# GpSimd's residual update at each sub-layer border placed behind VectorE's last add for the second token tile

## The reference

```python
for i in range(DEPTH):                                            # DEPTH = 2
    f1 = swiglu_ffn(rms_norm(h, ffn1_norm_pre[i]), ffn1_w_gu[i], ffn1_w_down[i])
    h = h + 0.5 * rms_norm(f1, ffn1_norm_post[i])
    u = rms_norm(h, mix_norm_pre[i])
    ...                       # four causal mixers (two attentions, two convolutions), gated and summed
    h = h + rms_norm(merged @ w_o[i], mix_norm_post[i])
    f2 = swiglu_ffn(rms_norm(h, ffn2_norm_pre[i]), ffn2_w_gu[i], ffn2_w_down[i])
    h = h + 0.5 * rms_norm(f2, ffn2_norm_post[i])
    pg = jax.nn.sigmoid(rms_norm(h, ple_norm_gate[i]) @ w_ple_gate[i])
    h = h + pg * rms_norm(p[i] @ w_ple[i], ple_norm_post[i])
```

## Time and profile before

| | |
|---|---|
| time, median of three runs | 1393.84 us (1391.57 to 1394.92) |
| span of the profiled execution | 1392.9 us, which is 0.94 us below that median |
| TensorE, matmuls | 1293.5 us busy, 93% of the span |
| VectorE | 823.9 us, 59% |
| ScalarE | 657.4 us, 47% |
| GpSimd | 254.2 us, 18% |
| mean granted TensorE clock | 0.975 |

### The profile page before, as it was taken

One profiled execution on the slowest core, in us unless ns is written; L12 is line 12 of the kernel. 1 busy time (PEld: TensorE's weight loads), 2 busy tenths in 40 slices (PEclk: granted clock), 3 DMA queues, 4 the chain that ended last, 5 costly groups with the idle time before them and its releaser, 6 DMA issues.

```text
span 1392.9 us, 17344 instructions
## 1 busy us (share of the span) xinstructions
PE 1293.5 (93%) x5972; PEld 1057.9 (76%) x5972; DVE 823.9 (59%) x767; ACT 657.4 (47%) x706; POOL 254.2 (18%) x210
## 2 busy tenths in 40 slices
PE   5299999899999989999969999989999998999996
PEld 4178887788778778888758888878887776888874
DVE  4154555455898765445656554564479886554464
ACT  3144444655645454444455444455664535444444
POOL 3030001310033460000433000040102256100015
PEclk9699999999999999999989999999999999999999
DMA  7675554635545446555257555555554544655641
GB/s 198 149 238 193 182 181 157 220 122 190 173 161 188 151 169 202 183 193 196 91 196 245 192 192 181 181 174 180 177 168 141 190 156 158 207 181 187 201 155 46
DMA packets 156842, 245.29 MB, mean 176 GB/s; under 512 B 9250, under 2 KB 108648, under 8 KB 156776
## 3 DMA queue, kind: packets, MB, share of 16 engines
q1 hardware_dynamic: 152280, 239.22, 51.4%
q0 software_dynamic: 1040, 2.10, 1.4%
q10 hardware_dynamic: 3456, 3.15, 0.8%
HBM read 241.29 MB, written 3.15 MB: 175 GB/s over the span
## 4 chain that ended last, share of the span: by engine, by line
PE 58%; issue 23%; POOL 6%; DVE 5%; DMA 4%; ACT 3%; SPq 0%; POOLq 0%; ACTq 0%; DVEq 0%
PE ps L1239 55%; DMA rel_scratch<-bandD 3%; PE ps L1286 3%; DVE hg L786 2%; POOL h L1139 1%; ACT whi L461 1%; DVE wlo L751 1%; POOL st L1134 1%; DVE hg L780 1%; POOL S L1139 1%; POOL st L1136 1%; DMA raw<-in_ffn_w_gu 1%; POOL hg L1139 1%; ACT gates L470 1%; ACT hg L470 0%
## 5 line engine op out<-in xcount | busy, mean ns | idle before, releaser
L751 DVE TENSOR_TENSOR wlo<-raw,whi 128x2048 fp32r<-128x2048 f32 (+1 forms) x216 | 507.5, 2352 | 348.4 <-ACT whi L461 181.4
L1239 PE MATMUL ps<-whi,xhi 128*128 128x512 f32 (+1 forms) x1280 | 502.9, 401 | 50.0 <-DVE S L795 32.9
L1239 PE MATMUL ps<-wlo,xhi 128*128 128x512 f32 (+1 forms) x1280 | 490.6, 391 | 0.0
L1239 PE MATMUL ps<-whi,xlo 128*128 128x512 f32 (+1 forms) x1280 | 490.4, 391 | 0.0
L1239 PEld LDWEIGHTS ps<-whi,xhi 128*128 128x128 f32 x1280 | 243.1, 191 | 106.6 <-DVE S L795 35.0
L461 ACT ACTIVATE whi<-raw 128x2048 fp32r<-128x2048 f32 (+1 forms) x120 | 225.7, 1884 | 146.6 <-PE ps L1239 98.2
L1239 PEld LDWEIGHTS ps<-whi,xlo 128*128 128x128 f32 x1280 | 243.8, 190 | 51.5
L1239 PEld LDWEIGHTS ps<-wlo,xhi 128*128 128x128 f32 x1280 | 244.4, 191 | 47.7
L467 ACT ACTIVATE whi<-raw 128x2048 fp32r<-128x2048 f32 x96 | 183.5, 1911 | 100.9 <-PE ps L1239 100.9
L1134 POOL TENSOR_TENSOR st<-st,epsc 128x1 f32<-128x1 f32 x36 | 28.3, 787 | 735.6 <-ACT hg L470 665.5
L1239 PE MATMUL ps<-whi,yhi 128*128 128x512 f32 x448 | 142.5, 393 | 1.2 <-DVE ylo L755 0.8
(11 more groups left out here) (127 smaller groups left out, 822.6 us busy)
## 6 DMA issues: line engine op xcount, KB each, us to landing
raw<-in_ffn_w_gu SPq DMA_DIRECT2D x176, 512.0 KB, 4.7
raw<-in_w_in SPq DMA_DIRECT2D x104, 512.0 KB, 4.4
raw<-in_ffn_w_down SPq DMA_DIRECT2D x88, 512.0 KB, 3.9
raw<-in_w_o SPq DMA_DIRECT2D x16, 512.0 KB, 3.6
raw<-in_w_ple_gate SPq DMA_DIRECT2D x16, 512.0 KB, 3.6
raw<-in_w_br_d SPq DMA_DIRECT2D x8, 512.0 KB, 3.6
gbias<-in_b_gate ACTq DMA_DIRECT2D x24, 128.0 KB, 3.1
raw<-in_w_in SPq DMA_DIRECT2D x8, 260.0 KB, 2.9
```

The source lines that it names most:

```text
L751: dve.tensor_tensor(d, a, b, ALU.subtract).then_inc(sem("lo_ready"), 1)
L1239: return nc.tensor.matmul(out_, lhsT, rhs, start=start, stop=stop, skip_group_check=True)
```

## The change

In `residual`, between the two factors of the post norm and the first `scale`, GpSimd now waits until VectorE has finished the last of its four adds of this border, the second half of tile 1. Nothing else is changed: no instruction is added or removed beside the wait.

```diff
@@ -1163,6 +1163,7 @@
                         tt(h[:, t, :], h[:, t, :], tmp[:, t, :], ALU.add, f"h{s}_{t}")
 
                     root(s)
+                    after(f"hg{e}_11")
                     scale(0)
                     add(0)
                     scale(1)
```

## The result

| | before | after |
|---|---|---|
| time, median (lowest to highest) | 1394.05 us (1391.57 to 1394.92), 4 runs | 1402.43 us (1400.86 to 1404.77), 4 runs |
| ratio, 95% interval | | 1.0069 (1.0054 to 1.0084) |
| span of the profiled execution | 1392.9 us | 1401.2 us |
| the same kernel once more, beside 23 runs of before | 1393.40 us | 1401.11 us, ratio 1.0058 (1.0045 to 1.0071) |

The change makes the kernel slower, by 7.7 us or 8.4 us between the medians of the two comparisons. The forecast was 1396.8, the range ended at 1400.6, and the chance given to slower was 0.28. In the experiments every run whose span was measured has a time 1.7 to 1.9 us above that span; so the profiled execution of before, with 1392.9, was by that one of about 1394.7, and not an execution 0.94 us quicker than the median.

The account below looks back on a forecast made before the run. TensorE's matmuls bound the kernel (93% busy), and GpSimd's list sets the last wait at the borders; +3.9 at A, -2.3 at B, +1.4 at C gave +3.0 us on the 1392.9 span, so 1396.8 us, range 1392.0 to 1400.6.

Parts of the forecast that it names:

- The list arithmetic: All borders: times of GpSimd's and VectorE's instructions stepped through, the engines excluding each other for whole instructions and taking turns.
- A, the list: Border A: GpSimd's add(1) ends 0.55 us late, so lo(36), TensorE's last wait in front of unit 36, comes late.
- A, the clock: Border A: the longer gap ahead of unit 36 drops TensorE's clock; 1.4 us each, taken between 1.1 and 1.9.
- B: Border B: add(1) ends 0.55 us late, but 1.7 us of slow clock comes back, in each of two layers.
- C: Border C: lo(105) and lo(106) back to back hold up the root's instructions; add(1) 0.7 us late, bounds 0.2 and 0.9.
- B's return: Border B: the slow stretch moves to where TensorE would wait anyway, so 1.7 us comes back; 0 if the clock falls again.
- two rows of shorter gaps: Profile rows behind the gaps ahead of 920.41 (border A) and 503.05 (border B): slow matmuls cost 1.1 and 1.9 us.
- the outer bound of twice the larger: Border A: the clock's cost bounded by nothing below and by twice the larger of 1.1 and 1.9 us above.
- Rival (c): Borders: lo does not keep GpSimd out of scale(1), chain ends 2.2 us earlier at each; -10 us, 1386.6; chance 0.1.
- "same" and "slower": Whole kernel: chances of a time within 0.3%, 4.2 us, of no change (0.61) and of a slower one (0.28).
- Rival (a): Clock charges at A and gives nothing back at B, or stays low for two stretches at A; +7.4, 1401.2; chance 0.25.
- Rival (b): Border A: the clock stays up, or charges little; +0.2 us in all, 1394.0; chance 0.15.

Follow-up runs that it names:

- fill kernel: Changed kernel plus 20 TensorE matmuls, results unused, in the gap in front of unit 36: 1397.36 us, ratio 1.0025 to the kernel before.
- the wait that is already over: Changed kernel with GpSimd's wait, at the same place, on tile 0's last add, which ended 4 us earlier: 1394.18 us, ratio 1.0000 to the kernel before.
- The waits at A, B and C measured alone: Changed kernel with the wait kept at one kind of border only: A 1401.80 us (1.0061), B 1395.28 us (1.0010), C 1395.56 us (1.0017).
- B alone: Changed kernel with the wait kept only at the two borders B: 1395.28 us, ratio 1.0010 (1.0000 to 1.0019) to the kernel before.
- wait behind scale(0): Changed kernel with the wait moved behind scale(0): 1392.89 us, ratio 0.9989; with ScalarE's order turned and SyncE's gain loads two chunks later too: 1378.88 us, 0.9899.

## Why the prediction was wrong

**What held.** The pair of adds takes 1.29 us in all borders (24 adds of 684 to 693 ns). scale(0) starts 2.8 us later than before against tile 1's fused multiply (2.75 foretold), scale(1) is held up by `lo(35)` (4.45 us against about 4.6 foretold), unit 36 comes 0.59 us late on the mean against 0.55, the gap in front of it is 4.93 us against "5 us", border C costs 0.9 us against 0.7, with both root instructions held up as chosen. The list arithmetic, one whole instruction at a time and the turns between the engines, came out within 0.2 us at every place named here. The Trainium skill ("SBUF — State Buffer", "SBUF: two separate sides") calls the shared ports an exclusive lock that a GpSimd instruction and a VectorE one with two SBUF inputs take for a whole instruction; the 4.45 us of scale(1) behind `lo(35)` and the 2.39 us of scale(0) beside the fused multiply, which has one input in PSUM, agree.

**The terms that were mis-sized.** By the stretches of the table above, in us for both layers:

| term | predicted | measured | by |
|---|---|---|---|
| A, the list | 2 x 0.55 | 2 x 0.59 | border A to unit 36 |
| A, the clock | 2 x 1.4 | 2 x 2.03 (1.45 to 2.6) | unit 36 to `D1a`; taken out in the fill kernel |
| B | 2 x (0.55 - 1.7) | 2 x -0.3 | five slow borders of eight |
| C | 2 x 0.7 | 2 x 0.9 | border C to the end |
| sum | +3.0 | +6.4 | |

The step that failed first is B's return, 1.7 us a layer, an error of 1.7 us in the sum: "Those 12 matmuls from 503.05 are slow now because the clock fell" was true of the one execution that was profiled, and taken for a property of the kernel. In that execution both borders B had the slow stretch, and it was a long one (about 1394.7 against a median of 1393.4); the forecast took the whole return off the median. Next, with 1.3 us, is the clock at A, taken between two rows of shorter gaps; the value measured lies above both, though inside the outer bound of twice the larger. With the measured terms the forecast would have been 1393.4 + 6.4 = 1399.8. That is still inside the range; what carried the measured times past its end of 1400.6 is the part that stays open below.

Three numbers of the prediction are off by themselves. The twelve matmuls from 503.05 cost 1.6 us more than fast ones by their starts (4.44 us against 2.86 with the clock up), not 1.9, as 4.61 holds the end of the last one too. Rival (c) takes its -10 from the forecast, although that sum already holds the +3.0; on the base it gives about 1383.6 and not 1386.6. The parts named for "same" and "slower" add up to 0.62 and 0.27, not 0.61 and 0.28.

Rival (a), that the clock charges at A and gives nothing back at B, was the nearest: +7.4, 1401.2, and its sum is within 1.3 us of both medians. It was right in size more than in mechanism, and so by some luck: against the execution profiled, B did give back about 1 us a layer. Rival (b) fell with the windows at 0.50, rival (c) with the 4.45 us.

**What stays open.** The terms explain 6.4 of the 7.7 to 8.4 us (the interval of the first comparison begins at 7.5 us, that of the second at 6.3). The stretch from `D1a` to border B took 77.3 us instead of 76.1 in two of six cases with the wait, but also in kernels without it, so I do not count it. The turn of the loop, from border C to the next border A, takes 233.6 us in the kernel before and 235.7 with the wait that is already over; in the other kernels it goes from 232.6 to 237.0. In the trace of after these two chances and the start add up to 3 us. The waits at A, B and C measured alone sum to 0.0088 against 0.0058 to 0.0069 together, and B alone at +1.0 per mille, where its stretches promise a gain of some 0.6 us, which lies outside its interval; all the intervals are too wide to say whether the terms interact. Moving SyncE's gain load at border C was not tried. Why the clock falls behind one gap and stays up behind another of the same length is not known either.

## What to carry to other kernels

Before an engine is made to wait so that another runs faster, find the last wait of the stretch and see whose list sets it: here the 14.3 us of TensorE's waits for the adds that the change removed came before waits that hung on GpSimd's list, and bought nothing. A wait against a port conflict belongs behind whatever the other engine's operation can run beside; one instruction later turned a loss of 6 per mille into a gain of 1 (0.2 to 2.0). Where a cost in a single profile is a clock state, look at the same place in the other layers and in kernels that don't touch it before it enters a sum as a constant; and a transfer that is hidden now has to be costed again in each version in which the stall that hides it is gone.

## What the runs showed of the hardware

- The length of a gap on TensorE does not decide alone whether the granted clock is at 0.50 behind it. In all 14 traces, for the gaps of 1.4 us and more that stand in front of weight units behind the borders, counted as fallen where matmuls within the first dozen behind the gap start 0.43 us apart instead of 0.23:

| gap, us | where | clock fell |
|---|---|---|
| 1.42 to 1.60 | border B | 0 of 11 |
| 1.82 to 1.84 | border C, unit 107 | 1 of 7 |
| 1.92 to 1.97 | border C, unit 107 | 0 of 8 |
| 1.97 to 2.16 | border B, tile 1, behind the stalled adds | 5 of 5 |
| 2.29 to 2.31 | border B, tile 1, wait behind scale(0) | 0 of 4 |
| 2.49 to 2.54 | border C | 5 of 12 |
| 2.61 to 2.64 | border A, unit 36 | 1 of 2 |
| 4.05 to 4.08 | border B, tile 0 | 12 of 12 |
| 4.93 to 4.97 | border A, unit 36 | 6 of 6 |

- A low stretch in front of tile 1 cost 1.5 us (the 2.0 between the two kinds of border B, less the 0.5 by which tile 1 was late).
- Behind the same gap of 4.93 us the low level lasted for 7 matmuls in one layer and for 12 in the other, and cost 1.45 and 2.6 us. The Trainium skill ("TensorE: Matmul & The Clock Gate", "What's actually happening") says that the number of slow matmuls varies from run to run for one kernel; here it varied from layer to layer in one run.
- GpSimd's one-column instruction takes 0.19 us or 0.55 us alone and up to 2.23 us or 2.48 us where VectorE's `lo` instructions stand back to back: the smallest operations on a list are the dearest ones to put beside a long one of the other engine.
